# Building the one-hots of the gate matrix from one 2048-element compare and one product, in the expert stage of a decoder block

## What is computed

```
top_v, top_i = lax.top_k(sc, PEER_TOPK)
cand_v = (top_v[:, :, 0, :, None] + top_v[:, :, 1, None, :]).reshape(t, PEER_HEADS, kk)
cand_id = (top_i[:, :, 0, :, None] * PEER_N_KEYS + top_i[:, :, 1, None, :]).reshape(t, PEER_HEADS, kk)
best_v, best_pos = lax.top_k(cand_v, PEER_TOPK)
expert = jnp.take_along_axis(cand_id, best_pos, axis=-1)
gate = jax.nn.softmax(best_v, axis=-1).astype(xn.dtype)
...
hc = jnp.einsum('cd,chkd->chk', xc, u[ec])
ac = gc * jax.nn.gelu(hc)
return jnp.einsum('chk,chkd->cd', ac, v[ec])
```

## Time and profile before

| | us |
|---|---|
| three runs | 3340.43, 3343.63, 3347.16 |
| their median | 3343.63 |
| the profiled execution | 3340.54 |
| its span in the profile, first to last instruction | 3338.7 |
| the gate-matrix stage on DVE, first to last one-hot instruction | 987.5 to 1215.3 |
| PE busy over the span | 3216.9 (96%) |
| DVE busy over the span | 2480.9 (74%) |
| DVE busy in one block of the stage, of 19.16 | 19.16 |
| granted TensorE clock, mean over the span | 0.989 |

### The profile page before, as it was taken

The page is one execution under the profiler, slowest core; times in us unless marked ns, Lnnn a source line. Parts: engine busy times, 40 slices in busy tenths (PEclk is TensorE's granted clock), DMA queues, the critical chain, the costliest instruction groups (busy, mean ns, idle before and its releaser), DMA issues.

```text
span 3338.7 us, 48188 instructions
## 1 busy us (share of the span) xinstructions
PE 3216.9 (96%) x17333; PEld 2994.6 (90%) x17333; DVE 2480.9 (74%) x3744; ACT 1111.0 (33%) x1411; POOL 535.9 (16%) x381
## 2 busy tenths in 40 slices
PE   7999999999988889999999999999999999999997
PEld 5777788898888779999999999999999999999785
DVE  6444434699979977878888887888888888885644
ACT  4224423222225543333333323333233333333432
POOL 2120000011143221111212111121211112110200
PEclk8999999999999999999999999999999999999998
DMA  3231122333356667878878787887878878773222
GB/s 139 86 126 47 54 88 96 110 110 110 110 184 223 236 242 269 295 281 285 300 274 298 270 293 281 283 302 266 298 273 286 291 278 303 272 250 120 97 93 101
DMA packets 230385, 694.37 MB, mean 208 GB/s; under 512 B 17328, under 2 KB 75184, under 8 KB 194864
## 3 DMA queue, kind: packets, MB, share of 16 engines
q1 hardware_dynamic: 188848, 418.77, 36.5%
q0 software_dynamic: 36864, 268.45, 22.6%
q10 hardware_dynamic: 4608, 6.29, 0.5%
HBM read 657.79 MB, written 35.65 MB: 208 GB/s over the span
## 4 chain that ended last, share of the span: by engine, by line
PE 62%; issue 18%; DVE 12%; DMA 5%; ACT 2%; POOL 1%; DVEq 1%; SPq 0%; POOLq 0%; ACTq 0%
PE bank L475 19%; PE bank L476 19%; PE bank L477 19%; DVE one_g L1521 3%; DMA raw<-in_u_t 3%; DVE w_lo L1191 2%; DMA raw<-in_v 1%; DVE row L1497 1%; ACT w_hi L865 1%; POOL picked L1755 1%; PE bank L567 1%; PE bank L568 1%; PE bank L590 1%; DVE one_j L1524 1%; DVE x_lo L1629 1%
## 5 line engine op out<-in xcount | busy, mean ns | idle before, releaser
L475 PE MATMUL bank<-x_hi,w_hi 128*128 128x384 f32 (+1 forms) x3024 | 1081.9, 358 | 36.2 <-DVE x_lo L1208 16.1
L476 PE MATMUL bank<-x_lo,w_hi 128*128 128x384 f32 (+1 forms) x3024 | 1070.3, 354 | 0.0
L477 PE MATMUL bank<-x_hi,w_lo 128*128 128x384 f32 (+1 forms) x3024 | 1070.1, 354 | 0.0
L865 ACT ACTIVATE w_hi<-raw 128x1024 fp32r<-128x1024 f32 (+1 forms) x668 | 689.2, 1049 | 909.0 <-DMA raw<-in_v 336.2
L1191 DVE TENSOR_TENSOR w_lo<-raw,w_hi 128x1024 fp32r<-128x1024 f32 (+1 forms) x638 | 766.5, 1218 | 201.7 <-ACT w_hi L865 192.6
L475 PE MATMUL bank<-a_hi,w_hi 128*128 128x384 f32 x2048 | 688.1, 336 | 14.3 <-DVE w_lo L1191 10.9
L476 PE MATMUL bank<-a_lo,w_hi 128*128 128x384 f32 x2048 | 685.7, 335 | 0.0
L477 PE MATMUL bank<-a_hi,w_lo 128*128 128x384 f32 x2048 | 685.6, 335 | 0.0
L475 PEld LDWEIGHTS bank<-x_hi,w_hi 128*128 128x128 f32 x3024 | 571.7, 189 | 87.1 <-DVE w_lo L1191 21.9
L477 PEld LDWEIGHTS bank<-x_hi,w_lo 128*128 128x128 f32 x3024 | 571.4, 189 | 39.2
L476 PEld LDWEIGHTS bank<-x_lo,w_hi 128*128 128x128 f32 x3024 | 572.0, 189 | 38.6 <-issue 1.2
(11 more groups left out here) (194 smaller groups left out, 2183.0 us busy)
## 6 DMA issues: line engine op xcount, KB each, us to landing
raw<-in_u_t SPq DMA_DIRECT2D x256, 512.0 KB
raw<-in_v SPq DMA_DIRECT2D x256, 512.0 KB
gate_matrix<-g_blk SPq DMA_DIRECT2D x12, 2048.0 KB, 10.7
g_tile<-gate_matrix SPq DMA_DIRECT2D x32, 768.0 KB, 10.5
raw<-in_w_o SPq DMA_DIRECT2D x32, 512.0 KB
raw<-in_w_q SPq DMA_DIRECT2D x32, 512.0 KB
raw<-in_w_gate SPq DMA_DIRECT2D x32, 512.0 KB
raw<-in_w_in SPq DMA_DIRECT2D x26, 512.0 KB
```

What stands on the lines that cost most here:

```text
L475: pe.matmul(out, w_hi[slot][:, blk, :], m_hi, start=first, stop=False)
L476: pe.matmul(out, w_hi[slot][:, blk, :], m_lo, start=False, stop=False)
L477: return pe.matmul(out, w_lo[slot][:, blk, :], m_hi, start=False, stop=last)
L865: act.activation(w_hi[slot][:, 8 * s:8 * s + n, :], raw[s][:, 0:n, :], ACT.Copy)\
```

## The change

The tensors are laid out anew: `hk_t` becomes one tensor of three parts, and `one_j` and the i half go together into `one_ij`, two buffers of 2x8x128. One `tensor_tensor` of 2048 elements compares `iota` with the i and the j of 8 tokens. DVE then waits for this instruction of its own (`oh_ij`), since the next reads what it wrote, and a `tensor_tensor` of 1024 elements multiplies the i half by the gates into `one_g`. Eight `tensor_scalar` and one `tensor_tensor` become two `tensor_tensor`. PE waits for `oh_g` alone; the j half is done by then.

```
-                pe.wait_ge(oh_j, q + 1)
...
-                        mm = pe.matmul(out[:, t * P:(t + 1) * P], one_j[s][:, o, :], one_g[s][:, o, :],
+                        mm = pe.matmul(out[:, t * P:(t + 1) * P], one_ij[s][:, 1, o, :], one_g[s][:, o, :],
...
-                        act.activation(hk_t[i][:, :], bank[i][:, 0:TD], ACT.Copy).then_inc(hk_ready, 1)
+                        act.activation(hk_t[:, i, :], bank[i][:, 0:TD], ACT.Copy).then_inc(hk_ready, 1)
...
             def one_hots(q, s, first=False):
-                o = [P, OH, NK]
+                o = [P, 2, OH, NK]
                 if not first:
                     dve.wait_ge(g_done, 2 * q - 2)
-                for t in range(OH):
-                    ins = dve.tensor_scalar(one_g[s][:, t, :], iota[:, :], column(hk_t[0], q * OH + t),
-                                            column(hk_t[2], q * OH + t), ALU.is_equal, ALU.mult)
-                ins.then_inc(oh_g, 1)
-                dve.tensor_tensor(one_j[s][:, :, :], iota[:, None, :].to_broadcast(o),
-                                  hk_t[1][:, bass.ds(OH * q, OH)].unsqueeze(2).to_broadcast(o), ALU.is_equal)\
-                   .then_inc(oh_j, 1)
+                dve.tensor_tensor(one_ij[s][:, :, :, :], iota[:, None, None, :].to_broadcast(o),
+                                  hk_t[:, 0:2, bass.ds(OH * q, OH)].unsqueeze(3).to_broadcast(o), ALU.is_equal)\
+                   .then_inc(oh_ij, 1)
+                dve.wait_ge(oh_ij, q + 1)
+                dve.tensor_tensor(one_g[s][:, :, :], one_ij[s][:, 0, :, :],
+                                  hk_t[:, 2, bass.ds(OH * q, OH)].unsqueeze(2).to_broadcast([P, OH, NK]), ALU.mult)\
+                   .then_inc(oh_g, 1)
```

More of the change, by code:

```diff
@@ L170, in build_block @@
         t_if = [at(f"t_if{i}", one + 53 * K + 256 * i, [P, TC, TOPK]) for i in range(2)]
-        hk_t = [at(f"hk_t{i}", one + 2 * K * i, [P, TD]) for i in range(3)]
-        one_g = [at(f"one_g{i}", one + (14 + 4 * i) * K, [P, OH, NK]) for i in range(2)]
-        one_j = [at(f"one_j{i}", one + (22 + 4 * i) * K, [P, OH, NK]) for i in range(2)]
+        hk_t = at("hk_t", one, [P, 3, TD])
+        one_ij = [at(f"one_ij{i}", one + (6 + 8 * i) * K, [P, 2, OH, NK]) for i in range(2)]
+        one_g = [at(f"one_g{i}", one + (22 + 4 * i) * K, [P, OH, NK]) for i in range(2)]
         g_blk = [at(f"g_blk{i}", one + (30 + 16 * i) * K, [P, NK, TB]) for i in range(2)]
@@ L274, in build_block @@
         oh_g = sem("oh_g")
-        oh_j = sem("oh_j")
+        oh_ij = sem("oh_ij")
         g_done = sem("g_done")
```

## The result

The changed kernel takes 3358.5 us, the median of six runs from 3354.98 to 3361.16. The kernel before, run beside it, has a median of 3344.33, also of six, from 3340.42 to 3348.09. The ratio is 1.0042 with a 95% interval from 1.0029 to 1.0055, so the change costs 10 to 18 us, 14 by the medians. It is slower, by more than a measurement can miss, and the forecast of 3360 was 1.5 us off.

What follows compares the result with a forecast made beforehand. DVE was taken to bound the stage; +7.7 us work, +9.6 wait and -0.7 POOL make +16.6, against the median of 3343.6 a forecast of 3360 us, range 3349 to 3370.

Steps and rivals of the forecast that it cites:

- The bound: In the changed stage, DVE sets the length of a block (19.16 us busy), PE having 15.6 us of its own work.
- The compare: The new tensor_tensor of 2048 elements on DVE takes 2.28 us recorded, 2.21 from start to start.
- The bare work: DVE's group without any wait takes 3.35 us against 3.19, +0.16 a group, +7.7 us over 48 groups.
- The wait: DVE's product waiting for its own compare costs 0.22 us in 40 groups and 0.10 in 8, 9.6 us.
- The pair of accumulations: Two DVE instructions of 2048 elements with a wait and register step between, read as a gap of 0.15 us.
- The rival of the free wait: DVE's product starts as early as without a wait: +7.0 us in all, 3350.6; chance 0.09.
- POOL's price: Each w_lo on POOL costs DVE 1.97 us during a compare, otherwise 2.19; 2.06 on average against 2.09, -0.7 us.
- The share of 0.62: The part of DVE's time that compares fill, used to average what a w_lo costs to 2.06 us.
- The sum: Over the run, +7.7 for work, +9.6 for the wait and -0.7 for POOL make +16.6 us.
- Whoever is second waits: DVE's two-input instructions and POOL's exclude each other, and the one that comes later is held.
- PE's clock: Rival: at 1.2 instead of 2.4 GHz PE becomes the bound, +10 us per block hit, 3370 to 3380; chance 0.06.
- The last sign of being wrong: In the changed profile, PE's granted clock in the stage under 1.00 would show the forecast wrong.

Runs made afterwards that it cites:

- the cut kernels: The kernel before and the changed kernel, each with POOL's w_lo in the stage covering 16 of its 1024 elements: 3301.71 and 3309.85 us.

## Why the prediction was right, point by point

- **The bound.** DVE set the block before and after. PE's idle time in a block grew from 2.9 to 4.3 us, near the 3 and 5 that were named, and the cut kernels show PE's own 15.5 us where 15.6 had been read.
- **The compare.** 2.28 us wherever it isn't held, as taken from the row product. The other row, 2.34, was not it.
- **The bare work.** A group of the first two blocks is 1010.40 - 1006.94 = 3.46 us with a wait of 0.11, so 3.35 without, +0.16 on 3.19, +7.7 us in all.
- **The wait.** 0.15 us in the loop and 0.04 outside, by forecast 0.15 and 0.03. (The sum as written, 4.84 - 2 x 2.34, gives 0.16.) The pair of accumulations was the right row, because its order has the same form: a sequencer step that carries the wait stands directly in front. The rival of the free wait fell with the kernel before and one wait more, +0.83 us a block.
- **POOL's price.** 1.98 for the held product and 2.16 for the held compare, forecast 1.97 and 2.19. That the mean came out right is partly luck. It rests on one of each in every block but the first, and not on the share of time that was argued: POOL's arrivals hang on ACT, and so on PE's groups, and come at the same place each time. The share of 0.62 also leaves the row product out of DVE's time; with it compares fill 0.55 of a block.
- **The sum.** +16.6 forecast; +17.2 in the stage, +14.2 between the medians with an interval of 10 to 18.
- **What was missed.** The forecast let POOL always have its turn at the end of the instruction that it meets. That held for all 24 `w_lo` of the changed kernel, but not for four of the 24 in the kernel with the compare in two. "Whoever is second waits" is too simple as well: in the earlier trace rows `w_lo` is recorded 0.10 us ahead of `one_j` and is the one held all the same. What decides in such a close case is open.
- **PE's clock.** The rival did not come up. The last sign of being wrong, a granted clock under 1.00 in the stage, did show in the first block, at 0.92; it means nothing there, since the kernel before has 0.91 in its own first block. In the eleven others it is 1.00.

## What to carry to other kernels

Fewer instructions is not less work. Eight small instructions, each a compare and a multiplication fused, took 2.06 us. Without them the compare has 1024 elements more (2.21 - 1.14 us) and a product of 1024 elements (1.14 us) is added, 2.2 us together. The product also brought a wait of the engine for itself, which costs 0.1 to 0.2 us each time where the engine is the bound. Before costing such a change, read the start-to-start times of the small instructions, and look for a pair with a wait between them.

Where two engines exclude each other, ask what the bound one would pay to do the work itself. Here that was 1.14 us for an instruction that cost it 2.09 as a neighbour's.

## What the runs showed of the hardware

**A long two-input instruction of DVE holds the indirect loads too.** The load takes 0.95 us on POOL beside the short instructions, 1.70 beside compares of 1024 elements and 2.76 beside one of 2048, always just behind the row product. Kernel before, then the one with the compare in two, then the changed one:

```profile
1064.50 0.95 POOL L1785 DMA_INDIRECT row<-in_u_rows,expert  x1 [5.50 <-DVE row L1497]
```

```profile
1088.97 1.70 POOL L1785 DMA_INDIRECT row<-in_u_rows,expert  x1 [4.70 <-DVE row L1496]
```

```profile
1089.49 2.76 POOL L1784 DMA_INDIRECT row<-in_u_rows,expert  x1 [6.00 <-DVE row L1496]
```

In the last, the compare of 1089.14 ends at 1091.42, and the load 0.83 us behind it, which is about its own length. With the compare in two, the load also ends 0.83 us behind the compare that it met (1088.62 + 1.21). It is the same 2.75 with `w_lo` on DVE, so it is not POOL's other work. It cost nothing here, since DVE never waited for a row in this stage.

**A waiting POOL instruction can be passed over many times.** For 8 us, from 1055.97 to 1063.99, DVE started one two-input instruction after another and POOL's stayed out. It happened to four of 24 `w_lo`, all of which came 0.2 to 0.3 us before the end of a compare; four others came in the same stretch and got their turn at its end. All four that were passed over came in behind a row product. That DVE's accumulator read there is what let them in is only inferred from the place.

**Without disturbance the price of a wait depends on the form.** The waiting instruction starts 0.03 to 0.04 us after the end of the one ahead where its addresses are fixed, and 0.12 (`one_j` with a wait more) to 0.15 (the product) where the sequencer has to compute them behind the wait. Against a start without a wait, which lies 0.07 before that end, this is a price of 0.10 and of 0.2.
